# Attention stage of a hybrid decoder step: VectorE's place for the cached sequence's chain, ahead of a step's mix in place of behind it

## The chip, the cores and the metric

One Trainium2 chip, one core of it. The metric is the time of one launch on the device, in microseconds (us), as the median of three runs. A profiled execution of the same program gives the trace; its rows are times in us from the start of its span. The engines are TensorE (PE, its weight loads PEld), VectorE (DVE), ScalarE (ACT), GpSimd (POOL) and SyncE (SP). Each runs its own queue in order, and they meet by semaphores alone.

## What is computed

One inference step of two layers for a prompt of 1024 positions and 8 sample sequences of 4 new positions. The change lies in the differential attention of the even layer, cut here to its core:

```python
def _diff_attend(q, k, v, q_pos, k_pos, lam):
    s = jnp.einsum('bqhmd,bkhmd->bhmqk', q, k).astype(jnp.float32) * (DH_B ** -0.5)
    mask = k_pos[None, :] <= q_pos[:, None]
    p = jax.nn.softmax(jnp.where(mask, s, -jnp.inf), axis=-1)
    a = p[:, :, 0] - lam * p[:, :, 1]
    return jnp.einsum('bhqk,bkhe->bqhe', a.astype(v.dtype), v)
...
# prompt: 4 heads, causal, blocks of 128 queries
# samples: k_all, v_all = 2048 cached positions (pages of 128, by page_table) + 4 new ones
k_past = cache_k[e][page_table].reshape(DEC_BATCH, PAST_LEN, H_B, 2, DH_B)
v_past = cache_v[e][page_table].reshape(DEC_BATCH, PAST_LEN, H_B, DV_B)
```

Two softmax maps are made for each head and block, and the second is taken from the first, weighted by lam. The rest of the step (retention, gated linear attention, two convolutional feed-forward blocks, norms, all projections) is not touched.

## The kernel before, in words

The whole step is one program of stages, each closed by a barrier of all engines. `stage_attention` (L2222) is one of them. It does two kinds of work side by side.

**The prompt's attention** runs in two passes of a loop (`i`, two heads each), and each pass in 16 steps `s`: for each of its two heads, 8 blocks of 128 queries. A step with block `qb` sees `(qb + 1) * 128` keys, so the width grows from 128 to 1024 columns and starts again with the second head. A step goes through these parts:

- TensorE `score` (L2370, rows L2380): two maps of scores into the bank `ps_s`, each written when ScalarE's exponential of the step before has read the same map (semaphore `exped`).
- VectorE `masked_max` (L2487): for each map the causal mask (L2494), the row maximum (L2496), and its negative (L2501) for ScalarE.
- ScalarE `exps` (L2602, rows L2614): two exponentials into `p` and `p2` with row sums. They wait for the maximum and for the step before's mix, since `p2` is single.
- VectorE `mix` (L2503): reciprocals of the sums (L2507, L2509), then over the whole width a product (L2511) and a product with a sum (L2513). The result is one map.
- TensorE `turn` (rows L2392) two steps later, ScalarE `take_turned` (L2622), TensorE `product` (rows L2402) three steps later, ScalarE `take_product` (L2627).

**The samples' attention** handles one cached sequence in each window of four steps (`WIN` = 4, `w = s % 4`, written w0 to w3 below; four windows in a pass, eight in all). Each engine does one part of it in each step:

- w0: TensorE `cached_scores` (L2412, L2423 into `bank_a`), VectorE `cached_max` (L2533 to L2539), ScalarE `cached_exps` (L2632, L2633).
- w1: VectorE `cached_sums` (L2543) at the head of the step, TensorE `cached_turns` (L2431 to L2435), ScalarE `cached_take` (two copies, L2638 and L2639, then after VectorE's difference an exponential, L2641), VectorE `cached_top` (L2553, L2555).
- w2: VectorE `cached_weights` (L2564 to L2569) at the head of the step, TensorE `cached_products` (L2446 to L2452), VectorE `cached_column` (L2574).
- w3: ScalarE `cached_scale` (L2646), TensorE `cached_picks` (L2459), VectorE `cached_output` (L2578). The next window's `cached_queries` (L2523, L2525) stand at the head of its w0.

The order of the work is written out by hand: each engine's block is a loop over steps. On TensorE a step is `score`, the turns and products of older steps, and the cached part last. On ScalarE it is `take_turned`, `cached_scale` in w3, `exps`, `take_product`, then `cached_exps` or `cached_take`. SyncE loads the next sequence's keys and part of its values, GpSimd the rest of its values (`values_behind`, L2350), both released by TensorE's cached work.

Of the kernel before, what the change touches and what calls it, by code (L numbers as in the profile page):

```python
# [2221 lines left out]
def stage_attention(nc, g, qkT, cache_k, cache_v, ids, kt, v_ahead, val, o):  # L2222
# [20 lines left out]
    with ExitStack() as stack:  # L2243
# [47 lines left out]
        def row_block(s):  # L2291

            return ROW_BLOCKS[s % NCH]
# [183 lines left out]
        def _(dve):  # L2477
# [9 lines left out]
            def masked_max(i, s):  # L2487
                qb = row_block(s)
                L = (qb + 1) * CH
                for m in range(2):  # L2490
                    link = i * (LINKS * STEPS) + (LINKS * s + 2 * m)
                    diag = ps_s[:, m, qb * CH:L]
                    dve.wait_ge(scored, i * (2 * STEPS) + (2 * s + m + 5))
                    nc.vector.tensor_tensor(diag, diag, g.col("causal"), ALU.add).then_inc(dv, 1)  # L2494
                    dve.wait_ge(dv, link + 1)
                    nc.vector.tensor_reduce(out=mx[:, m:m + 1], in_=ps_s[:, m, 0:L], axis=AX.X, op=ALU.max)\  # L2496
                        .then_inc(dv, 1)
                    dve.wait_ge(dv, link + 2)

                    dve.wait_ge(exped, i * (2 * STEPS) + (2 * s + m + 1))  # L2500
                    nc.vector.tensor_scalar(nm[:, m:m + 1], mx[:, m:m + 1], -SC, None, ALU.mult).then_inc(maxed, 1)  # L2501

            def mix(i, s):  # L2503
                L = (row_block(s) + 1) * CH
                link = i * (LINKS * STEPS) + (LINKS * s + 4)
                dve.wait_ge(exped, i * (2 * STEPS) + (2 * s + 4))
                nc.vector.reciprocal(rs[:], sums[:]).then_inc(dv, 1)  # L2507
                dve.wait_ge(dv, link + 1)
                nc.vector.tensor_tensor(rs[:, 1:2], rs[:, 1:2], g.lam[:, 1:2], ALU.mult).then_inc(dv, 1)  # L2509
                mine = p[s % 3][:, 0:L]  # L2510
                nc.vector.tensor_scalar(mine, mine, rs[:, 0:1], None, ALU.mult).then_inc(dv, 1)  # L2511
                dve.wait_ge(dv, link + 3)
                nc.vector.scalar_tensor_tensor(out=mine, in0=p2[:, 0:L], scalar=rs[:, 1:2], in1=mine, op0=ALU.mult, op1=ALU.add).then_inc(mixed, 1)  # L2513
# [7 lines left out]
            def cached_queries(i, r):  # L2521
                dve.wait_ge(c_scored, i * SEQS + (r + 1))
                nc.vector.tensor_copy(ckn[:], qkT[:, KBK:KBK + H, new_cols(i, r)])  # L2523
                for m in range(2):
                    last = nc.vector.tensor_copy(  # L2525
                        cqz[64 * m:64 * m + 64, :].rearrange("p (h c) -> p h c", h=H)[:, :, m * NS:(m + 1) * NS],
                        qkT[64 * m:64 * m + 64, QB:QB + H, new_cols(i, r)])
                last.then_inc(c_qready, 1)
# [12 lines left out]
            def cached_sums(i, r):  # L2541
                dve.wait_ge(c_exped, i * SEQS + (r + 2))
                nc.vector.tensor_reduce(out=cs[:], in_=csums[:], axis=AX.X, op=ALU.add).then_inc(c_sums, 1)  # L2543
# [14 lines left out]
            def cached_weights(i, r):  # L2558

                chain = cached_chain(i, r, 4)  # L2560
                dve.wait_ge(c_rexp, i * SEQS + (r + 1))

                dve.wait_ge(c_wcol, i * SEQS + (r + 1))
                chain.link(nc.vector.tensor_tensor(wrow[:], erow[:], rows(S_ROW), ALU.mult))  # L2564
                chain.link(nc.vector.tensor_reduce(out=total[:], in_=wrow[:].rearrange("o g r -> o r g"), axis=AX.X,
                                                   op=ALU.add))
                chain.link(nc.vector.reciprocal(total[:], total[:]))
                chain.link(nc.vector.tensor_tensor(total[:], total[:], coef[:], ALU.mult))
                nc.vector.tensor_tensor(wrow[:], erow[:], bc(total[:, None, :], [1, G, ROWS]),  # L2569
                                        ALU.mult).then_inc(c_weighted, 1)  # L2570
# [10 lines left out]
            with dve.Fori(0, H // 2) as i:  # L2581
                for s in range(STEPS):
                    r, w = divmod(s, WIN)
                    if w == 0:
                        cached_queries(i, r)
                    if w == 1:
                        cached_sums(i, r)
                    if w == 2:
                        cached_weights(i, r)
                    masked_max(i, s)  # L2590
                    mix(i, s)
                    (cached_max, cached_top, cached_column, cached_output)[w](i, r)

        @block.scalar
        def _(act):
# [1076 lines left out]
```

## Time and profile before

| what | value |
|---|---|
| time, median of 3 runs | 3141.92 us (3141.14 to 3144.3) |
| profiled execution | 3145.93 us, of which the span 3144.3 us |
| TensorE busy over the span | 2912.7 us (93%) |
| VectorE busy | 1493.6 us (48%) |
| ScalarE busy | 1080.5 us (34%) |
| GpSimd busy | 126.1 us (4%) |
| mean granted TensorE clock, of full speed | 0.951 |
| attention stage | about 499 to 754 us of the span |

A row of the trace in order of time has the start, the duration, the engine, the line, the operation with its tiles and shape, and in brackets how long the engine sat idle ahead of it and who released it. A busy share is an average over stages with different limits; for a change in one stage the rows of that stage count. The ends of TensorE's rows are modelled.

### The profile page before, as it was taken

How to read it: one execution, taken by the hardware profiler on the slowest of the kernel's cores; microseconds unless marked ns; L12 is line 12 of the kernel's file. 1: busy time of each engine (PE TensorE's matmuls, PEld its weight loads, DVE VectorE, ACT ScalarE, POOL GpSimd, SP SyncE). 2: the span in 40 equal slices, each digit the busy share in tenths (PEclk: the TensorE clock that was granted, in tenths of full speed). 3: DMA queues.
4: the chain of work that ended last, by engine and by line, in shares of the span. 5: the costliest groups of instructions: out<-in, count | busy, mean ns of one | idle time of the engine just before them, and what ended most of it. 6: DMA issues, size and time to landing. Idle time of an engine off the chain costs nothing. (4 is left out here: it accounts for less than half of the span.)

```text
span 3144.3 us, 50586 instructions
## 1 busy us (share of the span) xinstructions
PE 2912.7 (93%) x19526; PEld 2676.9 (85%) x19526; DVE 1493.6 (48%) x2326; ACT 1080.5 (34%) x2015; POOL 126.1 (4%) x192
## 2 busy tenths in 40 slices
PE   6999978888989999999998999787889999999996
PEld 4898964545979999999996999776789999999995
DVE  4244035565574445544458103364565444444546
ACT  4112112335553333233335213343544333333232
POOL 0000001110000000000000000350000000000000
PEclk9999988878999999999998999897899999999998
DMA  6333177873231111111113302343431111111113
GB/s 238 124 129 121 51 274 255 289 254 115 99 117 48 47 47 40 47 52 41 47 51 125 136 21 98 130 161 108 157 134 41 41 52 47 40 53 40 47 43 120
DMA packets 141574, 320.69 MB, mean 102 GB/s; under 512 B 13633, under 2 KB 78882, under 8 KB 133122
## 3 DMA queue, kind: packets, MB, share of 16 engines
q1 hardware_dynamic: 95570, 233.07, 21.0%
q10 hardware_dynamic: 40752, 69.09, 6.2%
q0 software_dynamic: 5120, 16.78, 1.4%
q8 instruction: 82, 1.34, 0.2%
q14 instruction: 50, 0.41, 0.0%
HBM read 273.25 MB, written 45.64 MB: 101 GB/s over the span
## 5 line engine op out<-in xcount | busy, mean ns | idle before, releaser
L251 PE MATMUL f_acc<-h_hi,f_hi 128*128 128x352 f32 x1488 | 482.6, 324 | 4.9 <-DVE h_lo L1766 4.3
L251 PE MATMUL f_acc<-h_lo,f_hi 128*128 128x352 f32 x1488 | 478.3, 321 | 0.0
L251 PE MATMUL f_acc<-h_hi,f_lo 128*128 128x352 f32 x1488 | 477.8, 321 | 0.0
L251 PE MATMUL f_acc<-m_hi,f_hi 128*128 128x352 f32 x1176 | 382.0, 325 | 4.9 <-DVE m_lo L1766 4.3
L251 PE MATMUL f_acc<-m_lo,f_hi 128*128 128x352 f32 x1176 | 378.4, 322 | 0.0
L251 PE MATMUL f_acc<-m_hi,f_lo 128*128 128x352 f32 x1176 | 378.0, 321 | 0.0
L251 PE MATMUL f_acc<-f_ghi,f_hi 128*128 128x352 f32 x1056 | 345.2, 327 | 5.5 <-DVE y L1863 5.5
L251 PE MATMUL f_acc<-f_glo,f_hi 128*128 128x352 f32 x1056 | 340.4, 322 | 0.0
L251 PE MATMUL f_acc<-f_ghi,f_lo 128*128 128x352 f32 x1056 | 340.0, 322 | 0.0
L1668 DVE TENSOR_TENSOR f_lo<-f_st,f_hi 128x1024 fp32r<-128x1024 f32 x174 | 210.7, 1220 | 254.9 <-ACT f_hi L1314 254.8
L1856 DVE TENSOR_TENSOR y<-y,f_acc 128x1056 f32<-128x1056 f32 x160 | 200.3, 1252 | 260.2 <-PE f_acc L251 260.2
L1822 DVE SCALAR_TENSOR_TENSOR f_cv<-f_up,vec,f_cv 128x1072 f32<-128x1072 f32 x88 | 117.3, 1333 | 356.8 <-ACT f_cv L1498 356.8
L251 PEld LDWEIGHTS f_acc<-h_hi,f_hi 128*128 128x128 f32 x1488 | 280.3, 188 | 5.9 <-DVE h_lo L1766 4.6
L251 PEld LDWEIGHTS f_acc<-h_lo,f_hi 128*128 128x128 f32 x1488 | 280.7, 189 | 0.5 <-issue 0.2
L251 PEld LDWEIGHTS f_acc<-h_hi,f_lo 128*128 128x128 f32 x1488 | 280.1, 188 | 0.0
L1484 ACT ACTIVATE f_up<-f_acc 128x704 f32<-128x704 f32 x86 | 65.4, 760 | 511.4 <-PE f_acc L251 511.4
L251 PEld LDWEIGHTS f_acc<-m_hi,f_hi 128*128 128x128 f32 x1176 | 221.8, 189 | 5.9 <-DVE m_lo L1766 4.6
L251 PEld LDWEIGHTS f_acc<-m_lo,f_hi 128*128 128x128 f32 x1176 | 222.1, 189 | 0.5 <-issue 0.2
L251 PEld LDWEIGHTS f_acc<-m_hi,f_lo 128*128 128x128 f32 x1176 | 221.7, 189 | 0.0
L251 PEld LDWEIGHTS f_acc<-f_ghi,f_hi 128*128 128x128 f32 x1056 | 199.0, 188 | 15.8 <-DVE y L1863 7.4
L251 PEld LDWEIGHTS f_acc<-f_glo,f_hi 128*128 128x128 f32 x1056 | 199.4, 189 | 0.2
L251 PEld LDWEIGHTS f_acc<-f_ghi,f_lo 128*128 128x128 f32 x1056 | 198.9, 188 | 0.0
(444 smaller groups left out, 5317.0 us busy)
## 6 DMA issues: line engine op xcount, KB each, us to landing
f_st<-w_ffn SPq DMA_DIRECT2D x132, 512.0 KB, 3.5
kt<-cache_k SPq DMA_DIRECT2D x96, 256.0 KB, 5.5
vt<-cache_v SPq DMA_DIRECT2D x64, 256.0 KB, 7.7
att_vt<-cache_v POOLq DMA_DIRECT2D x64, 256.0 KB, 6.6
gla_ada_w<-w_ada SPq DMA_DIRECT2D x14, 1024.0 KB, 6.8
x<-y ACTq DMA_DIRECT2D x9, 1408.0 KB, 6.2
ret_ada_w<-w_ada ACTq DMA_DIRECT2D x12, 1024.0 KB, 7.8
y<-w_qkv SPq DMA_DIRECT2D x10, 1024.0 KB, 6.1
```

Of the source, the lines that this page charges most:

```text
L251: last = nc.tensor.matmul(out, a(kk), b(kk), start=(n == 0), stop=(n == 3 * nk - 1))
L1484: nc.scalar.activation(up[x][:, 2:2 + 2 * TT].rearrange("p (n t) -> p n t", n=2), acc[x][:, 0:2, 0:TT], ACT.Copy)
L1668: nc.vector.tensor_tensor(lo[u % NSL][:], st[u % 2][:], hi[u % NSL][:].bitcast(F32), ALU.subtract).then_inc(made, 1)
L1822: nc.vector.scalar_tensor_tensor(out=cv[x][:, 2:], in0=up[x][:, 1:UC - 1], scalar=wv(1), in1=cv[x][:, 2:], op0=ALU.mult, op1=ALU.add).then ...
L1856: nc.vector.tensor_tensor(ym, ym, acc[u % 2][:, :, 0:TT], ALU.add).then_inc(down_taken, 1)
```

## The change

In VectorE's loop of the attention stage the call of the cached part and the call of `mix` change places. What stands at the head of a step stays there.

```diff
                     if w == 2:
                         cached_weights(i, r)
                     masked_max(i, s)
+                    (cached_max, cached_top, cached_column, cached_output)[w](i, r)
                     mix(i, s)
-                    (cached_max, cached_top, cached_column, cached_output)[w](i, r)
```

Only VectorE's queue differs; its instructions are as many as before, and the queues of TensorE, ScalarE, GpSimd and SyncE are the same. Three places show it. First VectorE in w0 of a window with 640 columns; `att_rs` and `att_p` belong to the mix, `att_cmx`, `att_cm` and `att_cnm` to the cached maximum. Before:

```order
 L2507 RECIPROCAL att_rs<-att_sums 128x2
 L2508 REGISTER_ALU
 L2509 TENSOR_TENSOR att_rs<-att_rs,lam 128x1
 L2511 TENSOR_SCALAR att_p<-att_p,att_rs 128x640
 L2512 REGISTER_ALU
 L2513 SCALAR_TENSOR_TENSOR att_p<-att_second,att_rs,att_p 128x640
 L2532 REGISTER_ALU
 L2533 TENSOR_TENSOR att_bank_b<-att_bank_b,const 128x4
```

And in the changed kernel, at the same place, the end of the cached maximum and what follows it:

```order
 L2539 TENSOR_SCALAR att_cnm<-att_cm 128x1
 L2507 RECIPROCAL att_rs<-att_sums 128x2
 L2508 REGISTER_ALU
 L2509 TENSOR_TENSOR att_rs<-att_rs,lam 128x1
 L2511 TENSOR_SCALAR att_p<-att_p,att_rs 128x640
 L2512 REGISTER_ALU
 L2513 SCALAR_TENSOR_TENSOR att_p<-att_second,att_rs,att_p 128x640
 L2543 TENSOR_REDUCE att_cs<-att_csums 128x1
```

The mix moved from ahead of L2533 to between L2539 and L2543, the sum at the head of the next step. Second, VectorE in w1 of the first window (256 columns), as a piece of the difference; `att_top` and `att_erow` are the cached top and difference, `att_wrow` the weights at the head of the next step:

```order
-L2507 RECIPROCAL att_rs<-att_sums 128x2
-L2508 REGISTER_ALU
-L2509 TENSOR_TENSOR att_rs<-att_rs,lam 128x1
-L2511 TENSOR_SCALAR att_p<-att_p,att_rs 128x256
-L2512 REGISTER_ALU
-L2513 SCALAR_TENSOR_TENSOR att_p<-att_second,att_rs,att_p 128x256
 L2553 TENSOR_REDUCE att_top<-att_bank_b 1x32
 L2555 TENSOR_TENSOR att_erow<-att_bank_b,att_top 1x128
+L2507 RECIPROCAL att_rs<-att_sums 128x2
+L2508 REGISTER_ALU
+L2509 TENSOR_TENSOR att_rs<-att_rs,lam 128x1
+L2511 TENSOR_SCALAR att_p<-att_p,att_rs 128x256
```

The mix moved behind the difference, directly ahead of the weights. Third, VectorE in w2 of the first window (384 columns); `att_cw` is the column copy. Before:

```order
 L2501 TENSOR_SCALAR att_nm<-att_mx 128x1
 L2507 RECIPROCAL att_rs<-att_sums 128x2
 L2508 REGISTER_ALU
 L2509 TENSOR_TENSOR att_rs<-att_rs,lam 128x1
 L2511 TENSOR_SCALAR att_p<-att_p,att_rs 128x384
 L2512 REGISTER_ALU
 L2513 SCALAR_TENSOR_TENSOR att_p<-att_second,att_rs,att_p 128x384
 L2574 COPY att_cw<-att_bank_a 128x1
```

And in the changed kernel:

```order
 L2501 TENSOR_SCALAR att_nm<-att_mx 128x1
 L2574 COPY att_cw<-att_bank_a 128x1
 L2507 RECIPROCAL att_rs<-att_sums 128x2
 L2508 REGISTER_ALU
 L2509 TENSOR_TENSOR att_rs<-att_rs,lam 128x1
 L2511 TENSOR_SCALAR att_p<-att_p,att_rs 128x384
 L2512 REGISTER_ALU
 L2513 SCALAR_TENSOR_TENSOR att_p<-att_second,att_rs,att_p 128x384
```

The copy, which waits for TensorE's cached products, now stands ahead of the mix.

## Rows read from the trace of the kernel before

**Rows 1.** Windows: busy us and instructions by engine, granted clock, DMA share, GB/s.
```profile
core 0: us, PE busy (x) PEld busy (x) DVE busy (x) ACT busy (x) POOL busy (x), PEclk, DMA share, GB/s
499.00:754.00 255.00, 223.40 (x1568) 122.18 (x1564) 155.35 (x462) 101.29 (x274) 34.47 (x64) 0.85 0.70 249
```

**Rows 2.** Waits, 499 to 752: who waited for whom, us, times, longest.
```profile
DVE att_bank_b L2533 <- PE att_bank_a L2423: 11.9, 6, 2.5
...
PE att_ps_s L2380 <- ACT att_p L2614: 9.2, 6, 4.0
```

**Rows 3.** Timeline, VectorE, w0 of the first pass's last window: start, us, row.
```profile
588.29 0.17 DVE L2533 TENSOR_TENSOR att_bank_b<-att_bank_b,const 128x4 f32<-128x4 f32 x1 [1.70 <-PE att_bank_a L2423]
...
590.73 0.15 DVE L2543 TENSOR_REDUCE att_cs<-att_csums 128x1 f32<-128x2 f32 x1 [1.09 <-ACT att_cpn L2633]
```

**Rows 4.** Timeline, VectorE and TensorE, w0 of the first pass's second window.
```profile
527.53 0.17 DVE L2507 RECIPROCAL att_rs<-att_sums 128x2 f32<-128x2 f32 x1 [0.95 <-ACT att_second L2614]
...
529.19 0.16 DVE L2533 TENSOR_TENSOR att_bank_b<-att_bank_b,const 128x4 f32<-128x4 f32 x1
...
527.53 0.60 PE L2423 MATMUL att_bank_a<-kt,att_cqz 128*32 128x512 f32 x2
```

**Rows 5.** Timeline, VectorE and TensorE, first step of the second pass.
```profile
631.65 0.17 DVE L2507 RECIPROCAL att_rs<-att_sums 128x2 f32<-128x2 f32 x1 [6.40 <-ACT att_second L2614]
...
634.94 0.16 DVE L2543 TENSOR_REDUCE att_cs<-att_csums 128x1 f32<-128x2 f32 x1 [1.09 <-ACT att_cpn L2633]
...
624.57 2.79 PE L2423 MATMUL att_bank_a<-kt,att_cqz 128*32 128x512 f32 x24
...
634.96 1.11 PE L2431 MATMUL att_bank_a<-const,att_cp 128*128 128x128 f32 x4 [2.07 <-ACT att_cpn L2633]
```

**Rows 6.** Timeline, three engines, w1 of the first window.
```profile
510.32 0.17 DVE L2507 RECIPROCAL att_rs<-att_sums 128x2 f32<-128x2 f32 x1 [0.63 <-ACT att_second L2614]
...
511.38 0.27 DVE L2553 TENSOR_REDUCE att_top<-att_bank_b 1x32 f32<-1x128 f32 x1
...
512.34 0.28 DVE L2564 TENSOR_TENSOR att_wrow<-att_erow,att_bank_b 1x128 f32<-1x128 f32 x1 [0.37 <-ACT att_erow L2641]
...
510.66 0.25 ACT L2639 ACTIVATE att_cpnT<-att_bank_b 4x128 f32<-4x128 f32 x1
...
512.72 0.62 PE L2446 MATMUL att_bank_b<-vt,att_cpT 128*32 128x512 f32 x2 [1.21 <-DVE att_wrow L2564]
```

**Rows 7.** Timeline, VectorE, end of a 512-wide mix and the row behind it.
```profile
522.74 0.75 DVE L2513 SCALAR_TENSOR_TENSOR att_p<-att_second,att_rs,att_p 128x512 f32<-128x512 f32 x1
523.41 0.17 DVE L2578 COPY y<-att_bank_a 128x16 f32 x1
```

**Rows 8.** Timeline, three engines, w1 and w2 of the second window.
```profile
535.68 0.17 DVE L2507 RECIPROCAL att_rs<-att_sums 128x2 f32<-128x2 f32 x1 [1.06 <-ACT att_second L2614]
...
538.50 0.28 DVE L2564 TENSOR_TENSOR att_wrow<-att_erow,att_bank_b 1x128 f32<-1x128 f32 x1 [0.37 <-ACT att_erow L2641]
...
536.19 0.25 ACT L2639 ACTIVATE att_cpnT<-att_bank_b 4x128 f32<-4x128 f32 x1
...
541.60 0.62 PE L2446 MATMUL att_bank_b<-vt,att_cpT 128*32 128x512 f32 x2
```

**Rows 9.** Timeline: VectorE and weight loads, third window; ScalarE, w3 of the second.
```profile
573.33 0.17 DVE L2507 RECIPROCAL att_rs<-att_sums 128x2 f32<-128x2 f32 x1 [0.74 <-ACT att_second L2614]
...
574.05 0.62 DVE L2513 SCALAR_TENSOR_TENSOR att_p<-att_second,att_rs,att_p 128x384 f32<-128x384 f32 x1
574.84 0.16 DVE L2574 COPY att_cw<-att_bank_a 128x1 f32<-128x1 f32 x1 [0.17 <-PE att_bank_b L2452]
575.89 0.30 DVE L2494 TENSOR_TENSOR att_ps_s<-att_ps_s,const 128x128 f32<-128x128 f32 x1 [0.89 <-PE att_ps_s L2380]
...
579.13 1.35 PEld L2380 LDWEIGHTS att_ps_s<-qkT 64*128 64x128 f32 x5 [0.57 <-ACT att_second L2614]
...
552.34 1.12 ACT L2614 ACTIVATE att_second<-att_ps_s,att_nm 128x1024 f32<-128x1024 f32 x1
```

**Rows 10.** Timeline, GpSimd: one sequence's eight value loads.
```profile
518.30 4.63 POOL L1957 DMA_DIRECT2D att_vt<-cache_v  x8 [10.63 <-PE att_bank_b L2452]
```

## Prediction

> **What bounds the kernel now.** I read the attention stage alone, because only VectorE's order in it changes. First its busy times: in the 255 us from 499 to 754 TensorE is busy for 223.4, VectorE for 155.35 and ScalarE for 101.29, at a mean granted clock of 0.85 [rows 1]. TensorE is the nearest to full, so VectorE's idle time counts only where TensorE ends up waiting for it. Then the waits: VectorE loses 11.9 us, in 6 of 8 sequences, waiting for the cached scores; TensorE in turn loses 9.2 us, in 6 places, until ScalarE's exponentials free the score bank [rows 2]. Then I went through the order of time and asked of each move: when does VectorE's next masked maximum start, and is TensorE late by it? A mix itself is wanted by TensorE only two steps later, so its lateness costs nothing; what it pushes on VectorE can.
>
> I call the four steps of a window w0 to w3. A window serves one cached sequence. The mix is 128 to 1024 columns wide: w0 has 128 or 640, w1 256 or 768, w2 384 or 896.
>
> **w0: the cached maximum goes ahead of the mix.** In the last window of the first pass (width 640) the cached maximum starts at 588.29, when its scores arrive, and the cached sum, the last thing ahead of the next masked maximum, comes at 590.73 after a wait of 1.09 for ScalarE [rows 3]. So the cached maximum ends at 590.73 - 1.09 = 589.64. Afterwards the mix stands behind it. A mix of 640 takes 527.53 to 529.19 = 1.66 us [rows 4], so the sum comes at 589.6 + 1.66 = 591.25: **+0.5 us**. The mix lay under the wait for the scores; now it lies under the wait for ScalarE, which is too short for it. TensorE waits for the exponentials behind that next maximum [rows 2], so I count it in full. Three of the four 640-wide steps waited for their scores in this way: +0.51 each.
>
> The fourth, in the first pass, had its scores early: TensorE's last product of them ends at 527.53 + 0.60 = 528.13, while the cached maximum starts at 529.19 without a wait, only because the mix holds VectorE [rows 4]. Its sum came 2.44 behind, as above, at 531.63. Afterwards the maximum starts at 528.2, the mix at 529.5 and the sum comes at 531.15: **-0.5**.
>
> At width 128 the mix is shorter than one of 256 columns, which takes 510.32 to 511.38 = 1.06 [rows 6], so it fits in the 1.09: three of the four such steps come out even, 0. The cover is ScalarE's cached exponentials; were it gone, each would cost up to 1.06. The fourth, the first step of the second pass, is special. TensorE has its cached scores at 624.57 + 2.79 = 627.36, but the page's exponentials come late, so the mix starts at 631.65 and the sum at 634.94, and TensorE waits 2.07 us for what follows [rows 5]. Afterwards the cached maximum is done inside VectorE's wait of 6.40, ScalarE goes from the page's exponentials straight to the cached ones, and the sum comes at 631.65 + 1.09 = 632.74: **-2.2 us** on VectorE and, through the 2.07, on TensorE.
>
> **w1: the top and the difference go ahead of the mix.** They need ScalarE's copies of the turned weights, which stand behind the step's exponentials. In the first window the mix starts at 510.32, the top at 511.38, the weights at 512.34 after a wait of 0.37; the copies end at 510.66 + 0.25 = 510.91 [rows 6]. Afterwards the top starts at 510.94 and the mix 0.96 - 0.37 - 0.08 = 0.51 behind (0.08 is how early VectorE starts an independent instruction, 523.41 against 522.74 + 0.75 [rows 7]); the exponential of the difference hides under the mix. The weights move by 0.62 + 0.51 - 0.96 = **+0.17 us**. TensorE waits 1.21 us for just this instruction [rows 6], so +0.17 reaches it, and likewise in the second pass's first window. In the other six windows ScalarE also stores a product first: copies end at 536.19 + 0.25 = 536.44 against a mix that starts at 535.68, so the shift is 0.79 + 0.51 - 0.96 = 0.34. But there TensorE comes to the cached products late, at 541.60 against weights that start at 538.50 [rows 8]: 0. Without that slack each costs 0.34.
>
> **w2: the column copy goes ahead of the mix.** This puts a wait for the cached products in front of a mix that ran during them; behind it on VectorE stand the mix and the next masked maximum. In the third window the mix took 573.33 to 574.05 + 0.62 = 574.67, ahead of the copy at 574.84; the next maximum began at 575.89, when TensorE had its scores [rows 9]. Afterwards the mix starts at 574.93 and the maximum 1.34 - 0.08 = 1.26 later, 576.19: **+0.30**. That step's second exponential follows, and TensorE, which stalls 0.57 for it [rows 9], stalls 0.30 longer. This holds for the four steps of 384. At 896 I bound the shift by the same 0.30; but there ScalarE goes to the second exponential, at 552.34, without any wait for VectorE [rows 9], so 0.
>
> One rule speaks against this move. In the trace a mix at 522.74 runs inside GpSimd's issue of eight value loads, 518.30 for 4.63 us, with no idle ahead of it [rows 7, 10]; I add nothing. The Trainium skill, "SBUF — State Buffer", section "Who interferes with whom", says that VectorE and GpSimd share a port pair, and that whichever starts first keeps it while the other blocks. By that rule the w2 mixes, which now meet that issue, would each pay up to one load's 4.63/8 = 0.58: 3.5 for the four of 384 and up to two of 896, 3145.8 in all. The row does not bear it out.
>
> **w3: the output copy goes ahead of the mix**, into the wait for exponentials: at most 0.1 us less, taken as 0. No instruction, DMA or semaphore count is added, and the other engines' queues, SyncE's and GpSimd's too, keep their order.
>
> **The sum along the path.** First pass: +0.17 and +0.30 in the first window, given back by -0.5 in the second; +0.30 in the third, +0.51 in the fourth: +0.8. Second pass: -2.2 + 0.17 + 0.30, then +0.51, +0.30, +0.51: -0.4. Together **+0.4 us**. The profiled execution took 3145.93 us, its span 3144.3; it would become 3146.3. The median of the runs shown is 3141.92, 4 us less; with the same sum, **3142.3 us**.
>
> **Bounds.** Were nothing absorbed and nothing gained (w0 4 x 0.51, w1 2 x 0.17 + 6 x 0.34, w2 8 x 0.30) it would be +6.8: 3148.7. With only the gains, -2.7: 3139.2. I take the sum, since each term rests on the row for its own place.
>
> **Rivals.** A measurement of this kernel can tell about 0.2%, 6.3 us, from no change.
> 1. *It pays at every w0.* Were the cached scores there each time, both the 0.95 ahead of the mix [rows 4] and the 1.09 behind the maximum would go: 8 x 2.04 = 16.3 saved, less 1.5 of w1 and w2 on the path: 3127. Two of eight sequences look like that; the 6 waits of [rows 2] speak against it. Chance 0.04.
> 2. *Slower through TensorE's clock.* Longer stalls ahead of its scores leave it idle more often, and its mean is 0.85 already, between levels of 1.2 and 2.4 GHz [rows 1]. A mean of 0.82 would cost 0.03 x 255 = 7.7 us, 3150; from a loss of 0.023 it decides the sign. For it: nine stalls grow by 0.2 to 0.5. Against it: the stall of 2.07 goes. Chance 0.10; the reverse, over 6.3 us faster, 0.02.
> 3. *Every shift lands* (3148.7): the slack of w1 and of the wide w2 isn't there. Chance 0.03.
> 4. *Nothing that can be seen*: VectorE is off the path throughout, 3141.9, within the forecast's range.
>
> **How the numbers follow.** The forecast, with rival 4 and the port rule, 0.81; rival 1 0.04, rival 2 0.10 and 0.02, rival 3 0.03. So faster 0.06, same 0.81, slower 0.13. The range runs from the gains alone less a microsecond, 3138, to the clock's 3150.
>
> **What would show it.** In the changed profile, at width 640 the cached sum follows the mix with no wait of 1.09 and stands 2.95, not 2.44, behind the start of the cached maximum; at w2 the wait for the products stands ahead of the mix and TensorE's 0.57 becomes 0.9; the 2.07 of the second pass is gone; the stage still lasts 255 us, to about 1. Wrong would be a 640-wide step that gets shorter though its scores came late, a mix that is longer beside GpSimd's issue, or a stage whose granted clock moves by over 0.02.

## The result and the profile after

The changed kernel takes 3152.88 us (median of 6 runs, 3148.95 to 3159.3), the kernel before, run beside it, 3141.53 us (6 runs, 3136.27 to 3147.75). The ratio is 1.0038, with a 95% interval of 1.0025 to 1.0050: 11 us slower, and above the range of the prediction.

The profiled execution of the changed kernel took 3148.95 us (span 3147.3), against 3145.93 (span 3144.3) before. The attention stage, which I take from the start of VectorE's MEMSET of line 2479 to the start of ScalarE's last copy to y, lasted 255.4 us before and lasts 261.7 after. Its windows, before (busy us and instructions by engine, granted clock, DMA share, GB/s):

```profile
497.80:753.20 255.40, 223.91 (x1568) 122.71 (x1568) 156.15 (x466) 101.01 (x273) 34.47 (x64) 0.85 0.70 248
```

and after:

```profile
497.50:759.20 261.70, 229.94 (x1568) 127.43 (x1568) 153.96 (x466) 101.24 (x274) 35.48 (x64) 0.83 0.69 242
```

TensorE runs the same 1568 instructions and is busy 6.0 us longer, while its idle time is unchanged: 255.40 - 223.91 = 31.5 us and 261.70 - 229.94 = 31.8 us. So the stage is not longer because TensorE waits more. It is longer because the same matmuls take longer, at a mean granted clock of 0.83 in place of 0.85 of full speed (its two levels are 1.2 and 2.4 GHz): of the stage, the trace has 77.5 us at the lower level before and 87.7 after. Cut into stretches of time, which don't hold quite the same work in the two, before:

```profile
528.00:558.00 30.00, 26.30 (x176) 16.00 (x176) 21.62 (x56) 12.57 (x30) 4.29 (x8) 0.83 0.86 316
...
588.00:618.00 30.00, 25.84 (x153) 16.25 (x150) 18.63 (x45) 13.49 (x32) 4.29 (x8) 0.86 0.78 283
618.00:648.00 30.00, 22.69 (x158) 10.94 (x157) 12.31 (x48) 7.96 (x24) 0.68 (x2) 0.74 0.55 177
...
708.00:738.00 30.00, 27.64 (x182) 13.78 (x180) 20.65 (x57) 12.75 (x33) 4.29 (x8) 0.83 0.39 141
738.00:753.20 15.20, 11.53 (x89) 9.43 (x85) 6.27 (x13) 6.43 (x14) 0.00 (x0) 1.00 0.01 2
```

and after:

```profile
528.00:558.00 30.00, 26.19 (x184) 15.85 (x180) 21.85 (x58) 13.38 (x34) 4.64 (x8) 0.89 0.92 336
...
588.00:618.00 30.00, 25.57 (x137) 14.83 (x138) 19.98 (x49) 12.89 (x31) 4.29 (x8) 0.80 0.74 266
618.00:648.00 30.00, 23.61 (x169) 13.24 (x169) 12.11 (x48) 8.64 (x26) 0.96 (x2) 0.81 0.59 194
...
708.00:738.00 30.00, 27.21 (x176) 13.46 (x172) 19.77 (x56) 12.82 (x33) 4.46 (x8) 0.77 0.38 141
738.00:759.00 21.00, 17.69 (x97) 13.86 (x93) 7.79 (x16) 6.42 (x14) 0.00 (x0) 0.76 0.00 0
```

The clock is better in two of these stretches (0.83 to 0.89, 0.74 to 0.81) and worse in three (0.86 to 0.80, 0.83 to 0.77, and 1.00 to 0.76 in the last, which ends with the stage); in the four left out it moves by 0.01 at most. What that does to one and the same work is seen in the last products of the stage. TensorE's timeline (start, us, row), before:

```profile
744.92 1.58 PE L2402 MATMUL att_ps_o<-att_aT,att_v 128*128 128x128 f32 x12 [0.90 <-ACT y L2627]
...
747.96 1.73 PE L2402 MATMUL att_ps_o<-att_aT,att_v 128*128 128x128 f32 x14
```

and after:

```profile
746.96 2.90 PE L2402 MATMUL att_ps_o<-att_aT,att_v 128*128 128x128 f32 x12 [0.64 <-ACT y L2627]
...
752.05 3.20 PE L2402 MATMUL att_ps_o<-att_aT,att_v 128*128 128x128 f32 x14
```

These two groups alone take 6.10 us in place of 3.31. The windows from the start of the first to the end of the second, before and after:

```profile
744.90:749.70 4.80, 4.10 (x35) 3.92 (x36) 2.14 (x4) 1.62 (x4) 0.00 (x0) 1.00 0.00 0
...
746.90:755.30 8.40, 7.67 (x35) 7.32 (x36) 2.09 (x3) 1.66 (x4) 0.00 (x0) 0.50 0.00 0
```

The same 35 instructions ran wholly at the upper level before and wholly at the lower one after.

Now the waits, which answer to [rows 2]. After:

```profile
DVE att_bank_b L2533 <- PE att_bank_a L2423: 31.6, 8, 5.1
...
DVE att_cw L2574 <- PE att_bank_b L2452: 18.8, 8, 3.6
...
DVE att_top L2553 <- ACT att_cpnT L2639: 13.9, 8, 1.9
...
PE att_ps_s L2380 <- ACT att_p L2614: 11.2, 6, 4.3
...
DVE att_rs L2507 <- ACT att_second L2614: 9.6, 10, 3.2
```

VectorE now waits for the cached chain ahead of the mix, as the order says: 31.6 us for the cached scores, not 11.9. TensorE's own wait for the exponentials grew from 9.2 to 11.2 us only, and other waits of TensorE shrank: its idle time as a whole is 0.3 us longer. Seen from TensorE, that is what the order costs.

### The profile page after: what moved, and what is told of

It reads as the page before. It is cut to its first block and busy times, and to the rows that moved or that the text cites. A ratio compares the mean times of both kernels' runs of the same rounds, so it can differ in the third digit from the quotient of the medians.

```text
span 3147.3 us, 50586 instructions
## 1 busy us (share of the span) xinstructions
PE 2915.8 (93%) x19526; PEld 2679.9 (85%) x19526; DVE 1491.1 (47%) x2326; ACT 1080.1 (34%) x2015; POOL 127.1 (4%) x192
```

## The experiments

Two theories stood against each other. **Order**: the loss is made of waits between the engines that my sum priced too low. **Clock**: the loss is time at 1.2 GHz. In its first form it said that longer idle stretches of TensorE bring that time; from w3_only on it said, more widely, that what moves TensorE's idle places does. Each kernel below was timed beside the kernel before on its chip, whose median was 3142.25, 3142.41, 3142.62 and 3143.32 us in the four groups. The expectations say "order theory" for my sum of the prediction.

### The parts alone

The changed kernel once more (after_again), and versions in which only the steps with one value of w take the cached part ahead of the mix (here w = 0):

```
+                    cached = (cached_max, cached_top, cached_column, cached_output)[w]
                     masked_max(i, s)
+                    if w == 0:
+                        cached(i, r)
                     mix(i, s)
-                    (cached_max, cached_top, cached_column, cached_output)[w](i, r)
+                    if not (w == 0):
+                        cached(i, r)
```

> The changed kernel unaltered, for a second profile and a firmer ratio. Theory 'order' (the sum of shifts on the path, as predicted): +0.4 us against the kernel before, and the attention stage, 255 us before, within 1 us of that. Theory 'clock' (longer idle stretches of TensorE in the stage lower its granted clock): +8 to +14 us, the stage 5 to 12 us longer at a mean granted clock in it of 0.84 or less, and more of its length at the lower of the two levels than in the kernel before.

> Only the step w0 (cached maximum) has its cached part ahead of the mix; w1, w2, w3 stay as before. Order: three 640-wide steps +0.5 each, the one with early scores -0.5, the first step of the second pass -2.2: -1.2 us in all. Clock: TensorE's stall ahead of the scores of the step after w0 grows from 1.2 to 1.7 us at width 640, so +3 to +8 us with a lower mean granted clock in the stage.

> Only the step w1 (top and difference) has its cached part ahead of the mix. Order: +0.17 us in each pass's first window and nothing elsewhere: +0.3 us. Clock: no stall of TensorE grows by more than 0.2 us, so also within 1 us of the kernel before.

> Only the step w2 (column copy behind the cached products) has its cached part ahead of the mix. Order: +0.30 us in each of the four windows of 384 columns, of which the second window's slack takes some: +0.6 to +1.2 us. Clock: TensorE's stall ahead of the second map's scores in w0 grows from 0.57 to 0.9 us, +3 to +8 us with a lower mean granted clock in the stage.

The other two runs of this kind, w3_only and an unchanged copy of the kernel before, came with the next group:

> The kernel before, with nothing changed, as a scale for the others. All theories: within 2 us of the kernel before. The stage between its first MEMSET (line 2479) and its last copy to y was 255.4 us in the profile of before at a mean granted clock of 0.85; here 253 to 258 us at 0.84 to 0.86. If it comes out at 260 us and 0.83, one profile of a kernel tells nothing of that stage.

> Only the steps with s % 4 == 3 take cached_output ahead of the mix. Sum by the order of the instructions: 0 (no wait of the path moves by more than 0.1 us), so within 1 us of the kernel before. Clock theory (what the order moves inside a step changes where TensorE idles, and by that how long it runs at its lower clock): TensorE's idle places stay, so within 2 us. Any change of order costs the same, by something that the order does not show: +3 to +8 us, as after w0_only, w1_only and w2_only.

| kernel | median, us | ratio to before (95%) | stage, us | its granted clock | TensorE idle in it, us |
|---|---|---|---|---|---|
| before (profile shown) | 3141.53 | | 255.4 | 0.85 | 31.5 |
| before_again | 3142.58 | 1.0009 (0.9998 to 1.0019) | 255.6 | 0.85 | 31.8 |
| w3_only | 3141.98 | 1.0003 (0.9993 to 1.0013) | 255.4 | 0.85 | 32.7 |
| w0_only | 3149.65 | 1.0022 (1.0008 to 1.0036) | 258.0 | 0.84 | 31.8 |
| w1_only | 3146.23 | 1.0012 (1.0002 to 1.0022) | 262.0 | 0.83 | 31.6 |
| w2_only | 3149.92 | 1.0018 (1.0007 to 1.0030) | 261.3 | 0.83 | 31.9 |
| after | 3152.88 | 1.0038 (1.0025 to 1.0050) | 261.7 | 0.83 | 31.8 |
| after_again | 3152.68 | 1.0033 (1.0020 to 1.0046) | 262.9 | 0.82 | 30.8 |

What follows: the stage is a steady measure (255.4, 255.6 and 255.4 us in three profiles whose order is the same on the path, 261.7 and 262.9 in two of the changed order), so the 6 to 7 us are real. Not every reordering costs: w3_only, which moves nothing on the path, costs nothing. But w0, w1 and w2 each cost 4 to 8 us by the median, where the order had -1.2, +0.3 and +0.6 to +1.2. Together they cost 10, less than their sum (7.4 + 4.0 + 7.7 = 19), though the intervals are too wide to call that shown. In each the idle time is what it was and the clock is lower. Of w0_only's 7.4 us the stage shows only 2.6; where the rest lies isn't known. The stage of w1_only, with the wait ahead of TensorE's scores at s % 8 == 6 at 1.23 us as before, is as long as that of the whole change in its profiled execution (3150.4 us, 4 above its median):

```profile
495.70:757.70 262.00, 230.36 (x1568) 125.56 (x1568) 155.30 (x466) 101.11 (x273) 34.94 (x64) 0.83 0.68 242
```

The order theory fell here, by w0 and w2. The clock theory in its first form missed too: it had w1 within 1 us.

### Work put into TensorE's idle places

If the clock is the cause, then holding it up must make the loss go. These versions put matmuls whose results nobody reads into places where TensorE waits; 30 of them (the expectation says 31), of 512 columns, in either order of VectorE:

```
+            def fill(bank, n):
+                for _ in range(n):
+                    nc.tensor.matmul(bank, g.ident(), qkT[:, KBK, 0:512], start=True, stop=True)
+
+            free, turns = ps_s[:, 0, 512:1024], ps_t[:].rearrange("p j t -> p (j t)")
...
+                    if s % NCH == 6:
+                        pe.wait_ge(aready, i * PASS_BT + (batch_at(s - 2) + 1))
+                        fill(turns, 2)
+                    if i == 1 and s == 1:
+                        fill(free, 5)
                     if s < STEPS:
                         score(i, s)
                     if 2 <= s < STEPS + 2:
                         turn(i, s - 2, 0)
+                    if s == STEPS + 2:
+                        fill(free, 2)
                     if s >= 3:
                         product(i, s - 3)
+                    if s == STEPS + 1:
+                        fill(free, 2)
                     if 2 <= s < STEPS + 2 and batches(s - 2) > 1:
                         turn(i, s - 2, 1)
+                    if (i, s) in ((0, 1), (0, 2)):
+                        fill(free, 4 - s)
+                    if s % NCH == 3:
+                        fill(free, 1)
```

> The kernel before, with 31 matmuls of 512 columns put into places where TensorE idles in this stage (ahead of the scores at s % 8 == 6, ahead of cached_turns and cached_products at s = 1 and 2 of the first pass, ahead of cached_picks at s % 8 == 3, ahead of the score at s = 1 of the second pass, and between the last two steps of a pass); their results go to PSUM that nothing reads before it is overwritten, so they add work and change no result. Clock theory: the granted clock of the stage rises from 0.85 to 0.90 or more and the time falls by 5 to 20 us, since each us at the lower clock costs up to half a us. If idling has nothing to do with the clock: the clock stays at 0.85 and the time rises by 0 to 6 us, the part of the 13 us of new matmuls that does not fit into the idle places.

> The changed kernel with the same 31 matmuls. Clock theory: the 10 us of the change are time at the lower clock, so with the clock held up after_filled comes within 3 us of before_filled, and more than 12 us below the changed kernel. Order theory (the loss is made of VectorE's waits in the steps themselves): 8 to 12 us above before_filled. If the clock stays as it was in both (0.85 and 0.83), the pair tells nothing between the two.

Measured: before_filled 3133.92 us (ratio 0.9977, 0.9966 to 0.9988), after_filled 3133.60 us (0.9976, 0.9964 to 0.9987). The stage's clock is 0.94 and 0.95. The 10 us between the two orders are gone, and both kernels are below the kernel before by 8 to 9 us, although TensorE has about 29 us more work (an estimate: 30 matmuls at the 0.96 us that one of them takes in the rows of after_fill_s6 below; the expectation's 13 us was too low). This is what the clock theory said, in both numbers. That the two orders come out alike is weaker evidence than that both get faster: where TensorE waited 1.23 us in one order and 1.66 in the other, two added matmuls of 1.98 us cover both waits, and with them a price of the order.

Next the 30 were split in the changed order: the 8 ahead of the scores at s % 8 == 6, where a wait had grown, and the other 22. With the same edit, 12 more places were filled in both orders (42 in all).

> The changed kernel with 8 of the added matmuls only: two ahead of the scores of the steps with s % 8 == 6, where TensorE's wait for ScalarE's exponentials grew from 1.24 to 1.66 us. If that longer wait is what drops the clock in the changed kernel: nearly all of the 10 us come back, 3140 to 3144 us, and the granted clock of the stage is back at 0.85. If the loss is the sum of idle places all over the stage: 8 of 30 matmuls give a quarter to a third of the way to after_filled, 3145 to 3149 us. If the other places alone do it: 3151 to 3154 us.

> The changed kernel with the other 22 matmuls only (ahead of cached_turns, cached_products and cached_picks, ahead of the second pass's score at s = 1, and in the last two steps of a pass). If the longer wait ahead of the scores at s % 8 == 6 drops the clock: 3148 to 3154 us. If the loss is the sum of idle places all over the stage: two thirds to three quarters of the way to after_filled, 3138 to 3142 us. If these places alone do it: 3133 to 3136 us.

> The kernel before with 42 added matmuls in place of 30: one more ahead of cached_picks at s % 8 == 7, one between the two scores at s = 8, one ahead of the last turn's wait for its copy, two more ahead of the second pass's first wait and two ahead of its cached_products. Clock theory: another 0 to 5 us below before_filled, since the clock there is already near 0.94; above it by up to 3 us where the added matmuls overrun their idle places.

> The changed kernel with the same 42 matmuls. Clock theory: with the clock near full speed in both, what is left between the two is the order of the instructions alone: by the sum +0.4 us against before_filled_more, by the profiles of before_filled and after_filled (stage 246.8 and 243.8 us) -3 us. Order theory: 8 to 12 us above before_filled_more.

Three more runs settled what the 8 do: the wait that comes with them without the matmuls (`fill(turns, 2)` taken out again), the 8 in the order of before, and the 8 in w1_only.

> after_fill_s6 without its matmuls: only the wait for the copy of the last turns ahead of the scores at s % 8 == 6 stays. If the matmuls in the idle place bring the 20 us (clock theory): no change against the changed kernel, 3150 to 3155 us. If the earlier wait on its own moves something on TensorE's queue: 3132 to 3142 us.

> The kernel before with the 8 matmuls ahead of the scores at s % 8 == 6. If those idle places set the clock whatever the order: the clock of the stage rises to 0.88 or more and the time falls to 3130 to 3137 us, within 3 us of after_fill_s6 (3132.4), so that the change costs nothing once they are filled. If only the changed order needs them: 3139 to 3143 us.

> w1_only (cached_top ahead of the mix at s % 4 == 1 alone, 3146.2 us) with the same 8 matmuls. w1 moves none of TensorE's starts for long by the sum (+0.3 us). If its loss too is time at the lower clock: within 3 us of before_fill_s6. If it is a wait that the sum missed: 3 to 6 us above before_fill_s6.

| kernel | added matmuls | median, us | ratio to before (95%) | stage, us | its granted clock | TensorE idle in it, us |
|---|---|---|---|---|---|---|
| before_filled | 30 | 3133.92 | 0.9977 (0.9966 to 0.9988) | 246.8 | 0.94 | 15.7 |
| after_filled | 30 | 3133.60 | 0.9976 (0.9964 to 0.9987) | 243.8 | 0.95 | 13.0 |
| before_filled_more | 42 | 3131.07 | 0.9964 (0.9952 to 0.9977) | 240.6 | 0.98 | 7.6 |
| after_filled_more | 42 | 3130.10 | 0.9960 (0.9947 to 0.9973) | 241.9 | 0.98 | 6.3 |
| after_fill_rest | 22 | 3141.18 | 0.9997 (0.9985 to 1.0009) | 253.8 | 0.90 | 19.0 |
| after_fill_s6 | 8 | 3132.40 | 0.9973 (0.9959 to 0.9986) | 246.6 | 0.90 | 24.3 |
| before_fill_s6 | 8 | 3139.19 | 0.9986 (0.9977 to 0.9995) | 253.8 | 0.86 | 26.2 |
| w1_fill_s6 | 8 | 3136.37 | 0.9983 (0.9972 to 0.9993) | 246.1 | 0.90 | 27.0 |
| after_wait_s6 | 0 | 3153.02 | 1.0037 (1.0024 to 1.0050) | 263.3 | 0.82 | 31.3 |

(The profiled execution of before_fill_s6 is its slowest, 3145.55 us.)

The stage's windows of the two fullest kernels, before_filled_more:

```profile
498.40:739.00 240.60, 233.04 (x1652) 123.36 (x1652) 155.49 (x466) 100.83 (x273) 34.46 (x64) 0.98 0.73 263
```

and after_filled_more:

```profile
490.40:732.30 241.90, 235.65 (x1652) 122.86 (x1652) 154.24 (x466) 101.56 (x273) 36.17 (x64) 0.98 0.73 262
```

With the clock at 0.98 in both, what is left between the two orders is +1.3 us by the stage and -1.0 us by the median, so nothing that can be told from 0 (with the waits in part covered, as said). Both lie 11.6 to 12.5 us below their kernel before, and after_filled_more, at 3130.10 us, has the lowest median of this study, though the two can't be told apart.

How few matmuls it takes is seen in after_fill_s6. Its stage:

```profile
495.10:741.70 246.60, 222.35 (x1584) 121.33 (x1584) 154.19 (x466) 101.52 (x274) 36.30 (x64) 0.90 0.72 257
```

and TensorE's timeline at the first of its four places; line 2372 is the added work, line 2386 the score:

```profile
530.57 1.98 PE L2372 MATMUL att_ps_t<-qkT,const 128*128 128x512 f32 x4
532.49 3.00 PE L2386 MATMUL att_ps_s<-qkT 64*128 64x512 f32 x8
```

Two matmuls of 512 columns (each shown as two instructions) take 1.98 us in a place where TensorE sat idle for 1.65. Four such places, 8 us of added work, shorten the kernel by 20 us, from 3152.7 to 3152.9 down to 3132.4. All three expectations for this run were above that. And the wait without the matmuls, after_wait_s6, changes nothing (3153.02): it is the work that does it, not the order of TensorE's queue.

The other 22 matmuls bring 11 to 12 us, inside what the theory of a sum over the stage said, and the 8 bring more than that sum: the places are not equal, and their effects don't add. before_fill_s6 shows the same from the other side: the 8 matmuls that bring 20 us in the changed order bring 4 in the order of before, where I had expected 6 or more if the place alone decided; the time lies in the range for "only the changed order needs them". w1_fill_s6 came out 2.8 us below before_fill_s6 (their intervals overlap), not 3 to 6 above it, which speaks for the 4 us that w1_only lost being time at the lower clock and not a wait that the sum missed.

## Why the prediction was wrong

**The step that failed** is the clock, which the sum of +0.4 us put at nothing: the forecast let the stage last 255 us, "to about 1", at an unchanged 0.85. The stage came out at 261.7 us and 0.83. The prediction had named the mechanism as rival 2, "Slower through TensorE's clock", with "a mean of 0.82 would cost 0.03 x 255 = 7.7 us, 3150", and gave it 0.10. That its 7.7 us comes near what the stage lost is luck, for the reasons by which it weighed this rival are not what decides. For it stood "nine stalls grow by 0.2 to 0.5": w1_only has no longer stall ahead of its scores, and its profiled stage is as long. "Against it: the stall of 2.07 goes" was true, and the clock around that place did rise (0.74 to 0.81, 618 to 648), but it fell in three other stretches. So the wrong assumption was that the clock follows how long TensorE idles: its idle time is 31.5 us before and 31.8 after.

**The size.** At full clock the 77.5 us at the lower level would have taken at best half as long, and so would the 87.7 of the changed kernel: 38.75 and 43.85 us given back at most. The difference is 5.1 of the 6.3 us by which the stage grew. The Trainium skill, "Matmul & The Clock Gate", section "Terms", gives the same rule (the penalty is about the throttled time, times one less the ratio of the clock), and the trace agrees with it here to about 1 us. An estimate from the same record, without any added matmul, is what each stage would have lasted less that time: 216.7 and 216.8 us for before and before_again, and 217.8, 216.7 and 215.2 for after, after_again and after_wait_s6 (92.4 and 96.1 us at the lower level in the last two). Nothing like 6 us is left for waits. For the gain of the filled kernels the rule is no forecast: from before to before_filled_more, with 9.5 us at the lower level, it would give 34.0 us, and the stage gained 14.8, since the 42 matmuls add about 40 us of work and the idle time gave up 23.9.

The timed runs carry their mean clock as well. The 128 runs of the kernel before have a mean of 0.9528 at 3142.2 us, the 23 runs of the changed order (after, after_again, after_wait_s6) 0.9500 at 3152.9: (1 - 0.9528) x 3142.2 = 148.3 us against 157.6, so up to 9.3 of the 10.7 us. The stage accounts for 6.3 to 7.9 of them in the profiles. Where the rest lies isn't settled: the three profiled executions of the changed order (3148.95, 3148.49 and 3149.62) lie 3 to 4 us below the medians of their runs, and that of the kernel before lies 4 above.

**The steps of the order held** to about 0.1 us in most places where the two traces can be compared.

- *w0 at width 640.* Forecast: no wait of 1.09, and the sum 2.95 behind the cached maximum. VectorE's timeline after, where [rows 3] stood before:

```profile
588.01 0.17 DVE L2533 TENSOR_TENSOR att_bank_b<-att_bank_b,const 128x4 f32<-128x4 f32 x1 [4.37 <-PE att_bank_a L2423]
...
589.27 0.15 DVE L2507 RECIPROCAL att_rs<-att_sums 128x2 f32<-128x2 f32 x1
...
590.12 0.89 DVE L2513 SCALAR_TENSOR_TENSOR att_p<-att_second,att_rs,att_p 128x640 f32<-128x640 f32 x1
590.92 0.15 DVE L2543 TENSOR_REDUCE att_cs<-att_csums 128x1 f32<-128x2 f32 x1
```

590.92 - 588.01 = 2.91, and no wait. TensorE's scores two steps on wait for ScalarE's exponentials behind the next masked maximum, before and after:

```profile
593.38 1.12 PE L2380 MATMUL att_ps_s<-qkT 64*128 64x512 f32 x2 [1.23 <-ACT att_p L2614]
...
593.53 1.12 PE L2380 MATMUL att_ps_s<-qkT 64*128 64x512 f32 x2 [1.66 <-ACT att_p L2614]
```

That is +0.43, forecast +0.51, and the wait grew by as much in all four steps of this width.

- *The first step of the second pass.* Forecast: the 2.07 goes, the sum 1.09 behind the start of the mix in place of 3.29 [rows 5]. After:

```profile
634.96 0.17 DVE L2507 RECIPROCAL att_rs<-att_sums 128x2 f32<-128x2 f32 x1 [3.24 <-ACT att_second L2614]
...
635.87 0.15 DVE L2543 TENSOR_REDUCE att_cs<-att_csums 128x1 f32<-128x2 f32 x1
```

0.91, and TensorE goes from its score into the cached turns without a wait. But the mix itself starts at 634.96, not at 631.65 [rows 5]. From the scores above to the cached scores of this step, before and after:

```profile
593.40:623.40 30.00, 26.12 (x153) 17.59 (x153) 15.28 (x38) 12.00 (x28) 4.29 (x8) 0.83 0.80 289
...
593.50:626.20 32.70, 28.96 (x151) 18.97 (x151) 15.23 (x38) 11.97 (x28) 4.29 (x8) 0.74 0.75 270
```

The lower clock had used up 2.7 us, more than this gain, before it came.

- *w1.* In the first window TensorE's wait for the weights is longer by 0.22, forecast +0.17; where [rows 6] had 1.21 stands

```profile
512.63 0.62 PE L2446 MATMUL att_bank_b<-vt,att_cpT 128*32 128x512 f32 x2 [1.43 <-DVE att_wrow L2564]
```

In the second pass's first window, priced alike, TensorE idles 1.07 us ahead of these products in place of 0.33. The granted clock from the scores to them is 0.77 there and was 0.50, so this one can't be set against the sum.

- *w2.* Forecast: the wait for the products stands ahead of the mix, the next maximum about 1.35 behind the copy. After, where [rows 9] stood:

```profile
574.32 0.16 DVE L2574 COPY att_cw<-att_bank_a 128x1 f32<-128x1 f32 x1 [1.89 <-PE att_bank_b L2452]
...
575.65 0.29 DVE L2494 TENSOR_TENSOR att_ps_s<-att_ps_s,const 128x128 f32<-128x128 f32 x1
```

1.33 behind, with the wait of 1.89 now ahead of it; TensorE's stall of 0.57 [rows 9] became 0.83, forecast 0.9, and so (0.83 or 0.84) in all four steps of 384:

```profile
578.87 0.50 PEld L2380 LDWEIGHTS att_ps_s<-qkT 64*128 64x128 f32 x4 [0.83 <-ACT att_second L2614]
```

- *The sum, +0.4 us*: TensorE's idle time grew by 0.3 us, and the two orders lie -1.0 to +1.3 apart at a clock of 0.98. Rivals 1 (3127) and 4 (3141.9) didn't come; rival 3 (3148.7) gives nearly the time of the profiled execution, 3148.95, but by waits that the trace doesn't show.

**The port rule** (the Trainium skill, "SBUF — State Buffer", section "Who interferes with whom") would have had VectorE pay up to 0.58 in each w2 mix, by the prediction's reading. The mixes beside GpSimd's loads keep the length of their second product, 0.62 us at 384 columns and 1.15 at 896. The row that the prediction set against the rule was weak: the product at 522.74 overlaps the issue, which ends at 522.93, by 0.19 us only [rows 7, 10]. It is GpSimd that shows something, in the profile after:

```profile
518.21 4.78 POOL L1957 DMA_DIRECT2D att_vt<-cache_v  x8 [10.85 <-PE att_bank_b L2452]
...
574.93 4.80 POOL L1957 DMA_DIRECT2D att_vt<-cache_v  x8 [25.46 <-PE att_bank_b L2452]
607.05 4.63 POOL L1957 DMA_DIRECT2D att_vt<-cache_v  x8 [27.32 <-PE att_bank_b L2452]
...
606.78 0.68 DVE L2511 TENSOR_SCALAR att_p<-att_p,att_rs 128x896 f32<-128x896 f32 x1
```

Its issue of eight loads grows from 4.63 to 4.8 us beside a mix of 384 columns, in w2_only too. Beside one of 896 it stays at 4.63, though there as well it starts inside VectorE's product. So the rule is not borne out as the prediction read it; a price of 0.16 us, off the path, is all that the trace shows, and why it comes at one width alone is open.

**Open** is what makes one order with 31 us of idle time run at 0.85 and another at 0.82 or 0.83. The runs show that the amount of idle time isn't it, and that work in four places decides 20 us; that it is where the idle time lies is what is left, and no run shows it directly. They don't give a rule by which the clock could be forecast from an order.

## What to carry to other kernels

Where the granted clock of a stage is below full speed, price the clock before the waits: a change that moves waits by tenths of a microsecond can cost many times that through the clock (10 us here against a sum of 0.4), and the sum over waits forecasts only what is left when the clock stays the same. To learn which of the two a result is, compare TensorE's busy time over the same instructions (6 us more here, with the idle time equal), and fill its idle places with throw-away matmuls in both versions: if both get faster though they do more work, and the difference goes, it was the clock. In this stage such matmuls are themselves a tuning step: 42 of them bring 12 us, where none of the five reorderings tried brought any.

## What the hardware showed that was not expected

- In a stage whose idle places last about 2 us or less, but for one of 4, and come to 31.5 us together, the granted clock is 0.85; with 7.6 us idle, in before_filled_more, it is 0.98. The Trainium skill, "Matmul & The Clock Gate", section "What's actually happening", says that "the default state is throttled, and activity releases the throttle"; the filled kernels agree. The amount of idle time alone doesn't give the clock: 31.5 us idle stands at 0.85 in before, 30.8 us at 0.82 in after_again.
- Eight matmuls, about 8 us of added work, make the changed kernel 20 us faster (3152.9 to 3132.4). In their four places the granted clock is 1.00.
- Much of the scatter between the runs of one kernel goes with the clock as well: over the 128 runs of the kernel before, time and mean clock have a correlation of -0.86, with 2.3 us for each 0.001 of the clock.
